# Softmax sums of a head pair: reciprocals spread on VectorE and transposed, instead of broadcast by matmuls

## The chip, the cores and the metric

One NeuronCore of a Trainium2 chip runs the whole program. The metric is the device time of one execution in microseconds. The kernel before was timed in three runs, with a median of 2175.9 us.

## The reference, cut to what matters

The program is three transformer layers over 512 tokens of width 1024, in float32. Each has an attention part of several heads of width 64 and a feed-forward part. What the change touches is the end of each head's softmax attention:

```
logits = q @ k.T (+ decay, + causal mask)          # [queries, keys] of one head
p = softmax(logits, axis=-1)                       # exp(logits - max) / sum
out = p @ v                                        # [queries, 64]
```

In the last layer a learned sink adds exp(sink - max) to the sum; there and in the heads over a memory of 256 tokens the rest is the same.

## The kernel before, in words

Heads are worked off in 22 pairs, in three stages: 8 pairs from about 60 to 270 us of the span (stage 1: two over the memory, six causal ones), 8 from about 700 to 870 us (stage 2, the same numbers) and 6 from about 1655 to 1780 us (stage 3, four windowed ones with sinks and two over the memory). Between the stages lie the feed-forward parts, which the change does not touch.

A pair is two heads x = 0, 1 and 512 queries, four blocks of 128. Its key blocks are grouped into units of up to 512 score columns (128 for the causal pairs of stage 2, 256 in stage 3), and `Pairs.run` (L890) gives TensorE its work in rounds, a software pipeline of three steps. In a round it issues the scores of one unit (`score`, L786), and then, by `older` (L881), the values of the unit scored two rounds ago (`values`, L845) and the turn of the unit scored one round ago (`turn`, L816: transposes of the exponentials in float32, L1732). When the unit whose values are due is its pair's last (`sealed`), the round also has the pair's sums (`sums`, L854). In stages 1 and 2 the sums stand first, ahead of the values; in stage 3, where every job has `spare` set, they stand last, behind the turn. Rounds are interleaved with the dense matmuls of the layer (`beat`, L445, which lets side work through at a set pace), and `after(n, ...)` puts a step on the other engines' lists n units of model time later. All engines walk the one list `steps` in order, each with its own instructions; waits are on counting semaphores.

For a pair, VectorE takes the row maxima (L1895, scaled at L1904), ACT the exponentials with their sums as an accumulated output into `PSTAT[:, x, 1, i]` (L2139), TensorE turns the exponentials into PSUM, and ACT and VectorE copy them back to SBUF (L2146 and L1917; where `spare` is set, ACT alone copies both heads). With the turn of the last unit `copies` (L828) first orders `recip` (L868, step `precip`) and then these copies, so that on VectorE the reciprocal (L1927) stands directly ahead of the copy L1917. It makes 128x8 numbers: per query row of a block, 2 heads x 4 blocks. The step `pbcast` (L1750) then brings them into the layout of the output, [64 dimensions of head x, 512 queries], by eight matmuls per pair: the stationary operand is a column of reciprocals broadcast to 64 columns, the moving one is the identity. ACT copies the result to one of three buffers TMP (step `pspread`, L2162), VectorE multiplies the values in PSUM bank 6 by it (step `pmul`, L1932), ACT and VectorE split the product into a high and a low part (L2151, L1935). The values of the next pair start once L1932 has read bank 6. PSTAT has two buffers, handed on by `pstats`; TMP's three by `tmp`.

Other instructions that the prediction speaks of: the split of the weights into two parts on ACT and VectorE (L2069, L1795), three units of four tiles ahead of their use (`split_to`, L525); the normalisation of keys (L1849) and its transposes (`qturn`, L1684); the dense matmuls with three terms for each tile (L1625 to L1627, L1643 to L1645).

Of the kernel before, what the change touches and what calls it, by code (L numbers as in the profile page):

```python
# [287 lines left out]
def program(nc, io):  # L288
    with ExitStack() as ctx:
# [25 lines left out]
        IDENT, ONES2 = CONST[:, 0:128], CONST[:, 128:130]  # L315
# [24 lines left out]
        TMP = [sb(f"TMP{i}", [128, T]) for i in range(3)]  # L340
# [42 lines left out]
        PSTAT = [sb(f"PSTAT{i}", [128, 2, 4, 4]) for i in range(2)]  # L383
        GATE = [sb(f"GATE{i}", [128, 4, 12]) for i in range(2)]
        PSA = ctx.enter_context(nc.psum_tensor("PSA", [128, 8, T], F32))
        PS = [PSA[:, i, :] for i in range(8)]
# [11 lines left out]
        done = Signals(nc, ctx, now)  # L398
# [89 lines left out]
        sq, tmp, cv, gf, ys, ss, pstats, pp, pt = (Slots(n, need) for n in (2, 3, 4, 2, 2, 2, 2, 4, 2))  # L488
        ring, aux_ring, att_ring, held = [0, 1], [6, 7], [2, 3, 4, 5, 7], set()

        def step(kind, key, **a):
            if (kind, key) in WARM:
                warm((kind, key), WARM[kind, key])
            steps.append(Step(kind, key, a))
            for name in RAISES[kind]:
                done.mark(name, key)
# [272 lines left out]
        class Pairs:  # L769
# [16 lines left out]
            def score(self, n, u):  # L786
                job, key, jkey = self.jobs[n], (self.id, n, u), (self.id, n)
                if u == 0:
                    pstats.take(jkey, [("pbcast.pe", jkey)])
                self.at[key] = t = Unit(job.units[u], pick_pair(att_ring), job.spare)  # L790
                held.update(t.banks)
                for x, b in enumerate(t.banks):
                    psum.take(("pscore", key, x), [("pexp.act", key + (x,))], b)
                step("pscore", key, job=job, u=u, t=t)
                S, tokens = PSTAT[pstats.of[jkey]], pstats.before[jkey]

                def rest():
                    need(job.roots[1] if job.roots else [])
                    for xs in ((slice(0, 2),) if t.joint else (slice(0, 1), slice(1, 2))):
                        step("pmax", key + (xs.start,), job=job, t=t, xs=xs, S=S, tile=key, before=tokens)  # L800
                    if job.sealed(u) and job.sink is not None:
                        step("psink", jkey, job=job, S=S, last=key + (0 if t.joint else 1,))
                    after(0.8 if job.spare else 0, exponents)

                def exponents():
                    free = []
                    for n_ in range(t.parts):
                        t.P.append(pp.take(("pp", key, n_), [("pturn.pe", key + (x,)) for x in range(2) if t.shared or x == n_]))
                        free += pp.before["pp", key, n_]
                    for x in range(2):  # L810
                        step("pexp", key + (x,), job=job, t=t, x=x, S=S, P=t.of(PP, t.P, x), before=tokens, src=PS[t.banks[x]],
                             turned=free, top=("pmax.dve", key + (0 if t.joint else x,)))
                after(0.4, rest)
                return 0.4 + 1.4 * t.width / 512
# [39 lines left out]
            def sums(self, n, i):  # L854

                jkey, ckey = (self.id, n), (self.id, self.jobs[n].chunk)
                need([("precip.dve", jkey)])
                aux = aux_bank(("pbcast", jkey), [("pspread.act", ckey)])
                step("pbcast", jkey, S=PSTAT[pstats.of[jkey]], bank=aux)

                def spread():
                    x = tmp.take(("pmix", ckey), [("pmix.dve", ckey)])
                    step("pspread", ckey, jkey=jkey, bank=aux, F=TMP[x], before=tmp.before["pmix", ckey])
                    after(0.1 if self.jobs[n].spare else 0.4, lambda: self.mix(n))
                after(0.3, spread)
                return 0.8

            def recip(self, n):  # L868
                job, jkey = self.jobs[n], (self.id, n)
                S = PSTAT[pstats.of[jkey]]  # L870
                step("precip", jkey, job=job, S=S, last=self.end(n))

            def mix(self, n):
                job, key = self.jobs[n], (self.id, self.jobs[n].chunk)
# [6 lines left out]
            def older(self, scored, turned):  # L881

                ends = turned and self.jobs[turned[0]].sealed(turned[1])
                late = ends and self.jobs[turned[0]].spare
                cost = self.sums(*turned) if ends and not late else 0
                cost += self.values(*turned) if turned else 0
                cost += self.turn(*scored) if scored else 0
                return cost + (self.sums(*turned) if late else 0)

# [411 lines left out]
        last, norm = norm, Norm("mix1", XT, "mix1")  # L1301
# [46 lines left out]
        for p in range(6):  # L1348
            w = places[p % 2]
# [23 lines left out]
        for gr in range(3):  # L1373
# [71 lines left out]
            for x in range(2):  # L1445
                p = 2 * gr + x
# [162 lines left out]
        def tensor(pe):  # L1609
            w = Once(pe)  # L1610
            for s in steps:
# [114 lines left out]
                elif k == "pturn":  # L1726
                    for t in a["before"]:
                        w.wait_ge(*done(*t))
                    w.wait_ge(*done("pexp.act", key))
                    for x in range(a["t"].width // 128):  # L1730
                        c = slice(128 * x, 128 * x + 128)
                        p = pe.transpose(a["out"][:, c], a["P"][:, c], IDENT)  # L1732
                    p.then_inc(done.sem("pturn.pe"), 1)
                elif k == "pvals":
                    job, tile = a["job"], a["t"]
                    if a["u"] == 0:
                        for t in psum.before["pvals", a["jkey"]]:
                            w.wait_ge(*done(*t))
                    for t in tile.copied:
                        w.wait_ge(*done(*t))  # L1740
                    for i, col, k0, nk, masks in tile.subs:
                        nb = nk // 128
                        for j in range(nb):
                            for x in range(2):
                                r = slice(64 * x, 64 * x + 64)
                                p = pe.matmul(PS[6][r, 128 * i:128 * i + 128], job.v[:, k0 // 128 + j, r],
                                              tile.of(PT, tile.PT, x)[:, col + 128 * j:col + 128 * j + 128], start=(j == 0),
                                              stop=(j == nb - 1))
                    p.then_inc(done.sem("pvals.pe"), 1)
                elif k == "pbcast":  # L1750
                    for t in psum.before["pbcast", key]:
                        w.wait_ge(*done(*t))
                    w.wait_ge(*done("precip.dve", key))
                    for i in range(4):
                        for x in range(2):
                            p = pe.matmul(PS[a["bank"]][64 * x:64 * x + 64, 128 * i:128 * i + 128],
                                          a["S"][:, x, 3, i:i + 1].broadcast_to([128, 64]), IDENT, start=True, stop=True)
                    p.then_inc(done.sem("pbcast.pe"), 1)
                elif k == "warm":
                    w.wait_ge(s_cb, 16)  # L1760
                    for t in psum.before["warm", key]:
                        w.wait_ge(*done(*t))
                    for _ in range(a["n"]):
                        pe.matmul(PS[a["bank"]][:, 0:384], IDB, CB[:, 0:384], start=True, stop=True)
                elif k == "centre":
                    out = PS[a["bank"]][:, :]
                    for t in psum.before["centre"]:
                        w.wait_ge(*done(*t))
                    w.wait_ge(*done("tap.dve", (1, 29)))
                    pe.matmul(out, ONES, CA[0], start=True, stop=False)  # L1770
                    pe.matmul(out, ONES, CA[1], start=False, stop=True).then_inc(done.sem("centre.pe"), 1)
                elif k == "spreadout":
                    out = PS[a["bank"]][:, :]
                    for t in psum.before["spreadout"]:
                        w.wait_ge(*done(*t))
                    w.wait_ge(*done("lnsquare.act", 0))
                    pe.matmul(out, ONES, SG[0], start=True, stop=False)
                    pe.matmul(out, ONES, SG[1], start=False, stop=True).then_inc(done.sem("spreadout.pe"), 1)

        def vector(dve):  # L1780
# [6 lines left out]
            for s in steps:  # L1787
# [130 lines left out]
                elif k == "precip":  # L1918
# [3 lines left out]
                    if a["job"].sink is not None:  # L1922
# [1 line left out]
                        dve.tensor_tensor(St[:, :, 1, :], St[:, :, 1, :], St[:, :, 2, :],  # L1924
                                          ALU.add).then_inc(v_in.sem, v_in.up())
                        w.wait_ge(v_in.sem, v_in.n)
                    dve.reciprocal(St[:, :, 3, :], St[:, :, 1, :]).then_inc(done.sem("precip.dve"), 1)  # L1927
                elif k == "pmul":
                    F = a["F"][:, :]
                    w.wait_ge(*done("pvals.pe", a["last"]))  # L1930
# [507 lines left out]
```

## Time and profile before

| | |
|---|---|
| median of three runs | 2175.9 us (2173.77 to 2177.2) |
| profiled execution | 2173.69 us, span 2171.9 us |
| granted TensorE clock, mean | 0.995 |
| TensorE busy (matmuls) | 2106.6 us, 97% |
| TensorE busy (weight loads) | 1749.7 us, 81% |
| VectorE busy | 1268.6 us, 58% |
| ScalarE (ACT) busy | 938.9 us, 43% |
| GpSimd busy | 33.9 us, 2% |
| DMA | 86 GB/s over the span |

Busy times of an engine are sums over its records. The records of consecutive instructions of one engine overlap, since they are pipelined: what an instruction costs its engine is read from the distance between its start and the next one's. PE are TensorE's matmuls and PEld its weight loads, which run ahead of the matmuls that they belong to. A float32 matmul has two records, a float32 transpose one. In an engine's rows an idle time stands in brackets, with the instruction that ended it; "issue" is idle time in which it waited for nothing that the profile shows. The granted clock is a share of 2.4 GHz.

### The profile page before, as it was taken

How to read it: one execution, taken by the hardware profiler on the slowest of the kernel's cores; microseconds unless marked ns; L12 is line 12 of the kernel's file. 1: busy time of each engine (PE TensorE's matmuls, PEld its weight loads, DVE VectorE, ACT ScalarE, POOL GpSimd, SP SyncE). 2: the span in 40 equal slices, each digit the busy share in tenths (PEclk: the TensorE clock that was granted, in tenths of full speed). 3: DMA queues.
4: the chain of work that ended last, by engine and by line, in shares of the span. 5: the costliest groups of instructions: out<-in, count | busy, mean ns of one | idle time of the engine just before them, and what ended most of it. 6: DMA issues, size and time to landing. Idle time of an engine off the chain costs nothing. (4 is left out here: it accounts for less than half of the span.)

```text
span 2171.9 us, 30675 instructions
## 1 busy us (share of the span) xinstructions
PE 2106.6 (97%) x11441; PEld 1749.7 (81%) x11441; DVE 1268.6 (58%) x2133; ACT 938.9 (43%) x1898; POOL 33.9 (2%) x71
## 2 busy tenths in 40 slices
PE   7999999999999898999999999999999889999999
PEld 7899777888889676788888888888888667888887
DVE  7655567737755775776477544344448856443542
ACT  7655444424445764543244343223344654322331
POOL 0000001000001000000000000000001000000000
PEclk9999999999999999999999999999999999999999
DMA  6221123332233011233322323323332112333332
GB/s 214 79 59 54 50 78 97 107 97 88 97 98 97 16 35 35 74 102 103 91 97 97 102 93 98 101 92 98 97 96 65 30 45 88 97 99 96 97 97 93
DMA packets 101669, 187.36 MB, mean 86 GB/s; under 512 B 11408, under 2 KB 12048, under 8 KB 101264
## 3 DMA queue, kind: packets, MB, share of 16 engines
q1 hardware_dynamic: 101520, 185.39, 27.6%
q8 instruction: 91, 1.49, 0.3%
q14 instruction: 58, 0.48, 0.1%
HBM read 183.25 MB, written 2.10 MB: 85 GB/s over the span
## 5 line engine op out<-in xcount | busy, mean ns | idle before, releaser
L1795 DVE TENSOR_TENSOR WL<-RAW,WH 128x512 fp32r<-128x512 f32 x681 | 458.7, 690 | 357.9 <-ACT WH L2069 336.5
L1625 PE MATMUL PSA<-HNh,WH 128*128 128x512 f32 x1440 | 563.8, 392 | 5.6 <-DVE HNl L1784 4.2
L1627 PE MATMUL PSA<-HNh,WL 128*128 128x512 f32 x1440 | 560.3, 389 | 0.0
L1626 PE MATMUL PSA<-HNl,WH 128*128 128x512 f32 x1440 | 560.3, 389 | 0.0
L2069 ACT ACTIVATE WH<-RAW 128x512 fp32r<-128x512 f32 x681 | 413.1, 625 | 312.7 <-PE PSA L1627 221.3
L1625 PEld LDWEIGHTS PSA<-HNh,WH 128*128 128x128 f32 x1440 | 270.3, 188 | 66.7 <-DVE HNl L1784 7.6
L1627 PEld LDWEIGHTS PSA<-HNh,WL 128*128 128x128 f32 x1440 | 270.3, 188 | 56.8
L1626 PEld LDWEIGHTS PSA<-HNl,WH 128*128 128x128 f32 x1440 | 270.3, 188 | 56.6 <-issue 1.2
L1625 PE MATMUL PSA<-Gh,WH 128*128 128x512 f32 x704 | 274.1, 389 | 2.1 <-DVE Gl L1964 2.1
L1626 PE MATMUL PSA<-Gl,WH 128*128 128x512 f32 x704 | 273.9, 389 | 0.0
L1627 PE MATMUL PSA<-Gh,WL 128*128 128x512 f32 x704 | 273.9, 389 | 0.0
L1818 DVE TENSOR_TENSOR PSA<-PSA,ACC 128x512 f32<-128x512 f32 x180 | 125.3, 697 | 118.3 <-PE PSA L1627 111.9
L1784 DVE SCALAR_TENSOR_TENSOR CV<-PSA,PAR,CV 128x511 f32<-128x511 f32 (+1 forms) x176 | 131.9, 749 | 77.9 <-ACT CV L2168 74.7
L1643 PE MATMUL PSA<-WH,HNh 128*128 128x256 f32 (+2 forms) x512 | 153.0, 299 | 12.6 <-DVE HNl L1784 7.2
L2186 ACT ACTIVATE Gh<-GF 128x512 fp32r<-128x512 f32 x88 | 55.7, 633 | 235.1 <-DVE GF L1962 235.1
L1625 PEld LDWEIGHTS PSA<-Gh,WH 128*128 128x128 f32 x704 | 132.1, 188 | 30.2 <-DVE Gl L1964 2.9
L1626 PEld LDWEIGHTS PSA<-Gl,WH 128*128 128x128 f32 x704 | 132.1, 188 | 27.5
L1627 PEld LDWEIGHTS PSA<-Gh,WL 128*128 128x128 f32 x704 | 132.1, 188 | 27.4
L1644 PE MATMUL PSA<-WH,HNl 128*128 128x256 f32 (+2 forms) x512 | 148.4, 290 | 0.0
L1645 PE MATMUL PSA<-WL,HNh 128*128 128x256 f32 (+2 forms) x512 | 148.2, 289 | 0.0
L2168 ACT ACTIVATE CV<-PSA,PAR 128x512 f32<-128x512 f32 x88 | 68.6, 780 | 181.0 <-DVE PSA L1818 181.0
L1784 DVE SCALAR_TENSOR_TENSOR XT<-PSA,XT 128x512 f32<-128x512 f32 x64 | 44.3, 692 | 142.4 <-PE PSA L1627 142.4
(255 smaller groups left out, 2439.0 us busy)
## 6 DMA issues: line engine op xcount, KB each, us to landing
RAW<-in_w SPq DMA_DIRECT2D x681, 256.0 KB, 2.6
XT<-in_x SPq DMA_DIRECT2D x8, 256.0 KB, 5.2
MT<-in_mem SPq DMA_DIRECT2D x2, 1024.0 KB, 6.9
out_x<-XT SPq DMA_DIRECT2D x8, 256.0 KB, 2.0
PAR<-in_par SPq DMA_DIRECT2D x1, 207.0 KB, 7.2
CB<-in_cb SPq DMA_DIRECT2D x1, 100.0 KB, 7.2
PAR<-in_par SPq DMA_DIRECT2D x1, 84.5 KB, 2.0
CONST<-in_const SPq DMA_DIRECT2D x1, 65.0 KB, 5.7
```

The source lines that it names most:

```text
L1625: pe.matmul(out, wh, xh, start=(a["start"] and c == 0), stop=False)
L1626: pe.matmul(out, wh, xl, start=False, stop=False)
L1627: p = pe.matmul(out, wl, xh, start=False, stop=ends)
L1643: pe.matmul(out, h[:, c], wh, start=(a["start"] and t % a["share"] == 0), stop=False)
L1644: pe.matmul(out, l[:, c], wh, start=False, stop=False)
L1645: p = pe.matmul(out, h[:, c], wl, start=False, stop=(a["stop"] and t % a["share"] == a["share"] - 1))
L1784: ins = dve.scalar_tensor_tensor(*x)
L1795: dve.tensor_tensor(l[:, :], r[:, :], h[:, :], ALU.subtract).then_inc(done.sem("split.dve"), 1)
L1818: dve.tensor_tensor(ps, ps, nm.acc, ALU.mult).then_inc(done.sem("scale.dve"), 1)
L2069: act.activation(h[:, :], r[:, :], ACT.Copy).then_inc(done.sem("split.act"), 1)
L2168: act.activation(CV[cv.of[key]][:, :], PS[a["bank"]][:, :], ACT.Identity, bias=par(f"cb{a['layer']}", a["idx"]), scale=par(f"cw{a['layer'] ...
L2186: act.activation(Gh[:, a["q"], :], G[:, :], ACT.Copy).then_inc(done.sem("gated.act"), 1)
```

## The change

The reciprocal writes 128x512 numbers in place of 128x8: each of the eight columns is spread over 64 columns of a TMP buffer by a broadcast input. Four transposes of 128x128 bring that into the output's layout, in place of the eight matmuls. TMP is now taken twice for each pair (by `recip` and by `spread`), PSTAT is free once the reciprocal has read it, and in `older` the sums are behind the values where they were ahead of them. Nothing else is changed.

```diff
--- before.py
+++ after.py
@@ -786,7 +786,7 @@
             def score(self, n, u):
                 job, key, jkey = self.jobs[n], (self.id, n, u), (self.id, n)
                 if u == 0:
-                    pstats.take(jkey, [("pbcast.pe", jkey)])
+                    pstats.take(jkey, [("precip.dve", jkey)])
@@ -856,7 +856,7 @@
                 need([("precip.dve", jkey)])
                 aux = aux_bank(("pbcast", jkey), [("pspread.act", ckey)])
-                step("pbcast", jkey, S=PSTAT[pstats.of[jkey]], bank=aux)
+                step("pbcast", jkey, inv=TMP[tmp.of["inv", jkey]], bank=aux)
@@ -868,7 +868,8 @@
             def recip(self, n):
                 job, jkey = self.jobs[n], (self.id, n)
                 S = PSTAT[pstats.of[jkey]]
-                step("precip", jkey, job=job, S=S, last=self.end(n))
+                i = tmp.take(("inv", jkey), [("pbcast.pe", jkey)])
+                step("precip", jkey, job=job, S=S, inv=TMP[i], before=tmp.before["inv", jkey], last=self.end(n))
@@ -882,8 +883,8 @@
                 ends = turned and self.jobs[turned[0]].sealed(turned[1])
                 late = ends and self.jobs[turned[0]].spare
-                cost = self.sums(*turned) if ends and not late else 0
-                cost += self.values(*turned) if turned else 0
+                cost = self.values(*turned) if turned else 0
+                cost += self.sums(*turned) if ends and not late else 0
                 cost += self.turn(*scored) if scored else 0
                 return cost + (self.sums(*turned) if late else 0)
@@ -1752,9 +1753,8 @@
                         w.wait_ge(*done(*t))
                     w.wait_ge(*done("precip.dve", key))
                     for i in range(4):
-                        for x in range(2):
-                            p = pe.matmul(PS[a["bank"]][64 * x:64 * x + 64, 128 * i:128 * i + 128],
-                                          a["S"][:, x, 3, i:i + 1].broadcast_to([128, 64]), IDENT, start=True, stop=True)
+                        c = slice(128 * i, 128 * i + 128)
+                        p = pe.transpose(PS[a["bank"]][:, c], a["inv"][:, c], IDENT)
                     p.then_inc(done.sem("pbcast.pe"), 1)
@@ -1924,7 +1924,11 @@
                         w.wait_ge(v_in.sem, v_in.n)
-                    dve.reciprocal(St[:, :, 3, :], St[:, :, 1, :]).then_inc(done.sem("precip.dve"), 1)
+                    for t in a["before"]:
+                        w.wait_ge(*done(*t))
+                    dve.reciprocal(a["inv"][:, :].rearrange("p (i x d) -> p i x d", i=4, x=2),
+                                   St[:, :, 1, :].rearrange("p x i -> p i x").unsqueeze(3).broadcast_to(
+                                       [128, 4, 2, 64])).then_inc(done.sem("precip.dve"), 1)
```

## Rows read from the trace of the kernel before

**Rows 1.** The page's head and the busy time of each engine.
```profile
span 2171.9 us, 30675 instructions
...
PE 2106.6 (97%) x11441; PEld 1749.7 (81%) x11441; DVE 1268.6 (58%) x2133; ACT 938.9 (43%) x1898; POOL 33.9 (2%) x71
```

**Rows 2.** Busy time by stretch: PE, PEld, DVE, ACT, POOL, clock, DMA share, GB/s.
```profile
60.00:300.00 240.00, 237.52 (x2002) 207.98 (x1999) 132.51 (x256) 127.66 (x329) 0.00 (x0) 1.00 0.21 61
700.00:880.00 180.00, 159.16 (x1204) 125.83 (x1202) 118.26 (x228) 108.50 (x285) 11.60 (x11) 0.97 0.11 32
1655.00:1790.00 135.00, 118.62 (x925) 89.27 (x924) 103.84 (x234) 77.31 (x203) 6.01 (x9) 0.97 0.13 38
```

**Rows 3.** TensorE's weight loads in order of time (start, duration), first pair: sums, values, turns.
```profile
75.48 0.85 PEld L1756 LDWEIGHTS PSA<-CONST,PSTAT 128*64 128x64 f32 x16
76.30 0.91 PEld L1746 LDWEIGHTS PSA<-PT,VMEM 128*64 128x64 f32 x16
77.38 0.86 PEld L1732 LDWEIGHTS PSA<-CONST,PP 128*128 128x128 f32 x8 [0.17 <-issue]
```

**Rows 4.** The same view around four transposes of another step.
```profile
133.72 0.46 PEld L1684 LDWEIGHTS PSA<-CONST,YB 128*128 128x128 f32 x4
134.15 0.19 PEld L1643 LDWEIGHTS PSA<-WH,HNh 128*128 128x128 f32 x1
```

**Rows 5.** Groups by line: duration in ns as min/median/max, first and last start.
```profile
L1756 PE MATMUL PSA<-CONST,PSTAT x352: 272/273/324, 75.5 to 1777.9; 128*64 128x128 f32 x176
...
L1927 DVE RECIPROCAL PSTAT<-PSTAT x22: 193/202/205, 71.5 to 1775.7; 128x8 f32<-128x8 f32 x22
...
L1836 DVE TENSOR_SCALAR SS<-SS x31: 158/165/189, 37.4 to 1721.8; 128x8 f32<-128x8 f32 x25, 128x16 f32<-128x16 f32 x6
```

**Rows 6.** Costliest groups of the page: the weights' low part on VectorE.
```profile
L1795 DVE TENSOR_TENSOR WL<-RAW,WH 128x512 fp32r<-128x512 f32 x681 | 458.7, 690 | 357.9 <-ACT WH L2069 336.5
```

**Rows 7.** VectorE in order of time around the first pair's reciprocal.
```profile
71.46 0.17 DVE L1904 TENSOR_TENSOR PSTAT<-PSTAT,QR 128x4 f32<-128x4 f32 x1
71.54 0.20 DVE L1927 RECIPROCAL PSTAT<-PSTAT 128x8 f32<-128x8 f32 x1
71.66 0.67 DVE L1917 COPY PT<-PSA 128x512 f32<-128x512 f32 x1
```

**Rows 8.** Stage 3, first pair: VectorE's reciprocal and TensorE's first sum.
```profile
1684.99 0.20 DVE L1927 RECIPROCAL PSTAT<-PSTAT 128x8 f32<-128x8 f32 x1
...
1685.93 0.20 PEld L1756 LDWEIGHTS PSA<-CONST,PSTAT 128*64 128x64 f32 x4 [0.17 <-issue]
```

**Rows 9.** Stages 1 and 2: reciprocals and first sums of three pairs; a wait for YK.
```profile
157.93 0.20 DVE L1927 RECIPROCAL PSTAT<-PSTAT 128x8 f32<-128x8 f32 x1
...
159.15 1.09 PE L1756 MATMUL PSA<-CONST,PSTAT 128*64 128x128 f32 x16
...
769.76 0.39 PEld L1684 LDWEIGHTS PSA<-CONST,YK 128*96 128x96 f32 x4 [0.58 <-DVE YK L1849]
...
813.80 0.20 DVE L1927 RECIPROCAL PSTAT<-PSTAT 128x8 f32<-128x8 f32 x1
...
814.20 1.09 PE L1756 MATMUL PSA<-CONST,PSTAT 128*64 128x128 f32 x16
...
866.27 0.19 DVE L1927 RECIPROCAL PSTAT<-PSTAT 128x8 f32<-128x8 f32 x1
...
867.32 0.88 PE L1756 MATMUL PSA<-CONST,PSTAT 128*64 128x128 f32 x12
```

**Rows 10.** Waits of TensorE, and two stretches behind them (columns as in rows 2).
```profile
712.43 0.42 PEld L1732 LDWEIGHTS PSA<-CONST,PP 128*128 128x128 f32 x4 [3.93 <-ACT PP L2139]
...
714.00:716.00 2.00, 2.00 (x13) 1.61 (x13) 1.93 (x4) 1.37 (x4) 0.00 (x0) 0.50 0.04 8
...
1714.00:1717.00 3.00, 3.00 (x21) 2.23 (x21) 1.36 (x7) 1.69 (x5) 0.00 (x0) 0.50 0.00 0
```

**Rows 11.** What TensorE (PE and PEld together) waited for before L1746: us, times.
```profile
  DVE TMP L1932: 7.7, 8
```

## The prediction

> **What bounds the kernel now.** I read the page's first part, then the busy time by stretches. TensorE is busy for 97% of the span [rows 1], and the three stretches in which the 22 pairs of heads run are 240, 180 and 135 us long; TensorE is busy for 237.5 of the first, but only 159.2 and 118.6 of the others, where VectorE is busy for two thirds and more [rows 2]. So TensorE's order of instructions is the time: every microsecond that one of its instructions takes, or waits, shows one to one, and VectorE costs nothing until something that TensorE needs is late. Then I read the instructions in order of time around each pair's end, on TensorE (to see what the sums and their neighbours take) and on VectorE (to see how soon after the reciprocal TensorE comes for something that stands behind it).
>
> **TensorE's part: what is removed.** A pair's sums are 8 matmuls with 64 columns of weights, 16 records; 22 pairs give the 352 records of their group [rows 5]. The sixteen take from 75.48 to 76.30, where the values start: 0.82 us [rows 3]. Four transposes of the same 128x128 float32 form, in another step, hold the engine from 133.72 to 134.15: 0.43 us [rows 4]. By the weight loads' starts that is 0.39 us less for a pair, by the matmuls' starts 0.5; I take 0.45, times 22: 9.9 us. A change between matmuls and transposes shows as an idle time of 0.17 us [rows 3]. In the first 16 pairs (stages 1 and 2) the sums now go between values and turns: values, then 0.17, then sums and turns without a gap, against values, 0.17, turns before: nothing changes. In the last 6 (the third stage) the sums already stood behind the turns, and stay there; only their form changes, and the 0.17 before them [rows 8] goes, and mostly the one behind them too: about 1.7 us together. **TensorE's saving: 11 to 12 us, taken as 11.5.** Without anything else the kernel would take 2162.2.
>
> **VectorE's part: what is added.** The reciprocal of 128x8 becomes one of 128x512. No row shows a reciprocal of that size. Any 128x512 instruction with two operands takes 0.69 us [rows 6], so 0.6 us from start to start is the least. But the small reciprocal is not like its neighbours: it takes 0.202 us where a tensor_scalar on 128x8 takes 0.165 [rows 5], and the instruction behind it starts 0.12 us after it, where the one behind a 128x4 tensor_tensor starts 0.08 us after [rows 7]. A longer pipeline alone would lengthen the record, not the distance to the next start. Read as work for each element, with some 0.07 us fixed: (0.12 - 0.07)/8 = 6.2 ns by the starts, and (0.202 - 0.157)/8 = 5.6 by the durations, where 1.04 ns is the rate of a plain instruction ((690 - 165)/504) [rows 5, 6]. 512 elements then take 2.9 to 3.3 us; I take **3.2 us from start to start, 3.1 more than now**. The rows leave 0.6 (all of the excess fixed) to 3.9 us (the starts are rounded to 0.01). I take the value of the rows and not the low end because both the duration and the distance carry the same excess. 22 x 3.1 is 68 us of VectorE. PSTAT's buffers come free a little earlier, and TMP's three buffers are now taken twice per pair; the buffer's last reader is a pair back, so I cost both at nothing: what covers it is that a pair lasts for many times the 0.6 us by which any of them comes later. No DMA is added or moved, and SP and POOL see nothing.
>
> **What stands behind the reciprocal.** In stages 1 and 2 it is the copy of the transposed probabilities (L1917, 0.69 us), which the pair's last values need. The values now go where the sums started. So TensorE waits wherever its first sum started less than 3.2 + 0.69 = 3.9 us after the reciprocal did. Distances in the 16 pairs, in order of time: 3.9, 3.9, 2.2, 1.2, 5.5, 1.5, 3.0, 2.5, 2.0, 1.0, 2.1, 3.1, 3.8, 0.4, 2.1, 1.1. The first stands in [rows 3, 7] (71.54 to 75.48), two more and the last in [rows 9]: 157.93 to 159.15, a stall of 2.7 us; 813.80 to 814.20, 3.5; 866.27 to 867.32, 2.8. The sum over the 16 is 24.6 us. In one pair the chain behind the reciprocal is worse than its copy: TensorE already waited for VectorE's YK at 769.76 [rows 9], so the whole 3.1 us comes through there and not 0.7: 2.3 more. In the third stage ACT makes the copies, but the sums themselves wait for the reciprocal's 3.2 us; distances 0.9, 2.0, 3.0, 3.0, 3.5, 1.5 (the first: 1684.99 to 1685.93 [rows 8]): 5.9 us. **Direct stalls: 32.8 us.** The weight splits behind it on VectorE are ordered three units of weights (twelve tiles) ahead, and I let that hide them; without that cover they would wait as long as the copies do.
>
> **Second terms.** The sums' copy to SBUF (L2162) and the product (L1932) come about 0.6 us later in stages 1 and 2, since the values go first. TensorE waited 8 times for L1932 [rows 11]: about 2 us more. The clock: behind a wait of 3.9 us the granted clock was 0.50 for a stretch at 714 us, which is 1.2 of 2.4 GHz, and it was 0.50 again from 1714 us, behind several shorter ones [rows 10]. Stalls of about 3 us will do this at a few more places; a stretch of 2 to 3 us at half speed gives back 1 to 1.5. I take 5 us, bounds 0 and 12. Against this, waits for the exponentials that stand now behind some of these places shrink: 4 us off. **Sum: 32.8 + 2 + 5 - 4 - 11.5 = 24.3 us slower.** The profiled execution took 2173.7 (its span of 2171.9 and 1.8 around it); the median of the three runs is 2.2 above it. 2173.7 + 24.3 = 2198, 2200 by the median; I say **2199**.
>
> **Rivals.**
> (a) Cheap reciprocal, and so faster. The excess of 0.04 us is fixed for each instruction, and 128x512 takes 0.6 to 0.7 us. Place: VectorE, line 1927. The distances under 0.6 + 0.69 = 1.3 are then four, with 1.5 us of stalls together, and the later product costs 2: 11.5 - 3.5 = 8 gained, 2166. It decides below about 1.7 us a reciprocal, where stalls and saving cancel. For it: 8 elements are a short lever for 512. Against it: the distance to the next start has grown as well. Chance 0.14.
> (b) Dearer reciprocal: eight times the plain rate, 8 x 1.04 = 8.3 ns an element, 4.3 us. Each of the stalls grows by 1.1 us and three more pairs stall, about 24 us more: 2223. Against it: 8 elements would then have cost 0.058 us more than a plain instruction, and 0.04 was seen. Chance 0.11. The Trainium skill (VectorE: DVE Perf Modes, the section on the pipeline walkthrough) says that Reciprocal is an iterative divide on two of the eight slices with a repeat count of 8. By that rule, read as eight cycles an element, (b) would be the forecast; the trace's small reciprocal agrees with the direction and not with the full eight.
> (c) Right price, but TensorE finds it hidden: VectorE's copies catch up because the waits of one stall push back what competes with the next, and half of the 32.8 us is not seen; no clock lost. 16 + 2 - 4 - 11.5 = 3: 2178. For it: VectorE is busy for only 55% of stage 1. Against it: the distances are between two instructions that nothing else separates. Chance 0.11.
> That the change moves no values is no rival: TensorE runs its steps in the order written.
>
> **How the numbers follow.** The forecast's case (2 to 3.9 us a reciprocal, stalls seen) has 0.64 and by itself runs from about 2184 to 2215. 0.2% is about 4.3 us, which is what a measurement of this kernel can tell from no change. Faster: (a) and little of (c), 0.16. Within: part of (c), 0.06. Slower: 0.78. The range of 8 in 10 starts in (c), at 2176, and ends at 2222, just short of (b)'s middle.
>
> **What would show it.** The reciprocal's group: near 3.2 us a record (0.7 for (a), 4.3 for (b)). Transposes in place of the sums: 88 records, about 0.43 us for four, placed behind the values. TensorE's idle time before L1746 with VectorE's PT as its releaser: near 25 us in stages 1 and 2, where the product is the only releaser worth the name now [rows 11]; and before the sums of the third stage some 6 us with TMP as releaser. More stretches with a clock of 0.50 in stage 2. VectorE's total near 1335 us. The prediction is wrong if the reciprocal's record is under 1.7 us, or if it is about 3 and TensorE's idle time has not grown by more than 12 us.

## The result, and the profile after

Four runs of the changed kernel have a median of 2224.0 us (2223.2 to 2226.2), beside 2174.8 us for four runs of the kernel before: a ratio of 1.0226, 95% interval 1.0214 to 1.0239. The change costs 49 us; the forecast was 24, and 2224 lies just above its range. The profiled execution took 2224.45 us.

The page's head and busy times of the changed kernel, to be held against [rows 1]:

```profile
span 2222.7 us, 30151 instructions
...
PE 2115.4 (95%) x11177; PEld 1755.0 (79%) x11177; DVE 1334.9 (60%) x2133; ACT 938.4 (42%) x1898; POOL 34.8 (2%) x71
```

VectorE has 66 us more, as forecast (1335). TensorE executes 264 instructions fewer and is nevertheless busy for 9 us longer. The busy times by stretch (columns as in [rows 2], stages 1 to 3, somewhat longer stretches since the stages are) tell why: the granted clock of stages 2 and 3 fell to 0.91, and in stage 1, where it stays at 0.99, TensorE is idle for 14.3 us of 240 instead of 2.5.

```profile
60.00:300.00 240.00, 225.72 (x1854) 197.41 (x1852) 147.86 (x242) 122.82 (x322) 0.00 (x0) 0.99 0.21 58
700.00:900.00 200.00, 163.61 (x1106) 130.62 (x1104) 139.71 (x229) 110.70 (x292) 12.03 (x11) 0.91 0.10 29
1680.00:1820.00 140.00, 115.37 (x846) 89.42 (x845) 120.19 (x241) 75.75 (x200) 9.86 (x14) 0.91 0.13 37
```

The new reciprocal's group (ns min/median/max):

```profile
L1929 DVE RECIPROCAL TMP<-PSTAT x22: 3342/3353/3354, 71.0 to 1825.0; 128x512 f32<-128x512 f32 x22
```

VectorE in order of time around the fourth pair's reciprocal, the pair of 157.93 and 159.15 in [rows 9]:

```profile
160.12 3.35 DVE L1929 RECIPROCAL TMP<-PSTAT 128x512 f32<-128x512 f32 x1
163.39 0.63 DVE L1917 COPY PT<-PSA 128x512 f32<-128x512 f32 x1
```

and TensorE's weight loads behind it, values and transposes:

```profile
164.13 1.58 PEld L1747 LDWEIGHTS PSA<-PT,VP 128*64 128x64 f32 x16 [2.68 <-issue]
166.04 0.72 PEld L1757 LDWEIGHTS PSA<-CONST,TMP 128*128 128x128 f32 x4 [0.33 <-issue]
```

The copy starts 3.27 us after the reciprocal (160.12 to 163.39) and the values start 4.01 us after it, 2.68 us after TensorE was ready: the stall that the forecast gave this pair (2.7). The view calls the releaser "issue" for the weight loads and PT L1917 for the matmuls of the same records. The sixteen loads then take 1.58 us where they took 0.91 in [rows 3]: from 164 to 166 us the granted clock was 0.56, half clock for most of that stretch. The waits of TensorE's weight loads by line and releaser (us in total, times, longest), after:

```profile
PEld PSA L1747 <- issue: 27.8, 20, 4.0
PEld PSA L1733 <- ACT PP L2143: 24.3, 37, 3.9
...
PEld PSA L1713 <- DVE PT L1917: 9.4, 7, 2.7
...
PEld PSA L1757 <- DVE TMP L1929: 6.8, 4, 2.6
...
PEld PSA L1713 <- DVE HNl L1784: 4.0, 3, 1.8
...
PEld PSA L1747 <- DVE TMP L1936: 3.7, 3, 2.1
PEld PSA L1685 <- DVE YK L1849: 3.7, 1, 3.7
...
PEld PSA L1713 <- DVE AOL L1784: 3.4, 1, 3.4
PEld PSA L1757 <- issue: 3.4, 15, 0.3
...
PEld PSA L1747 <- DVE PT L1917: 2.0, 1, 2.0
```

and before, from the same view (lines one lower; L1746 are the values, L1732 the turns, L1712 the scores, L1684 the Q and K turns):

```profile
PEld PSA L1732 <- ACT PP L2139: 21.6, 37, 3.9
...
PEld PSA L1746 <- DVE TMP L1932: 4.3, 4, 2.0
...
PEld PSA L1712 <- DVE PT L1917: 3.6, 5, 1.5
...
PEld PSA L1712 <- DVE HNl L1784: 2.6, 3, 1.2
...
PEld PSA L1746 <- issue: 2.6, 9, 0.4
...
PEld PSA L1684 <- DVE YK L1849: 1.7, 2, 1.1
...
PEld PSA L1712 <- DVE AOL L1784: 0.4, 1, 0.4
```

**Two accounts.** For each kernel I take TensorE's idle time (the span less its busy time) and, from the view of busy times in stretches of 1 us, its "clock loss", the sum of (1 - granted clock) x busy time: what its busy time would shrink by at the full clock of 2.4 GHz. Before: 65.3 idle, 9.1 clock loss. After: 107.3 and 28.8. The rest, TensorE's work at full clock, went from 2097.5 (2106.6 - 9.1) to 2086.6. So +42.0 idle, +19.7 clock loss and -10.9 of work are the 50.8 us by which the spans differ. This account says where the time lies, not what it would give back.

Work hangs together by stage; where a stage ends is read from the first matmul of the next normalisation's total (L1668 before, L1669 after). All kernels of this case; the medians are of all their runs, the other columns of one profiled execution each, which can lie a few us from its median (e3's was the fastest of ten runs, e13's the slowest of eleven, 2175.5 us):

| kernel | median us | stage 1 ends | stage 2 ends | stage 3 ends | idle | clock loss |
|---|---|---|---|---|---|---|
| before | 2174.8 | 308.7 | 898.6 | 1819.4 | 65.3 | 9.1 |
| after | 2224.0 | 318.5 | 936.1 | 1870.2 | 107.3 | 28.8 |
| e1_order_only | 2178.2 | 307.9 | 902.4 | 1823.2 | 66.5 | 11.0 |
| e2_form_only | 2215.4 | 313.4 | 930.7 | 1862.8 | 100.8 | 25.9 |
| e3_copy_spread | 2176.9 | 304.5 | 898.3 | 1819.8 | 72.8 | 12.3 |
| e4_pool_spread | 2174.7 | 305.6 | 901.2 | 1822.5 | 69.1 | 20.4 |
| e5_form_copy | 2176.4 | 304.9 | 896.4 | 1821.0 | 70.3 | 16.8 |
| e6_dummy_block | 2230.5 | 319.5 | 939.3 | 1875.4 | 110.8 | 32.3 |
| e7_copy_first | 2212.7 | 310.8 | 921.6 | 1855.9 | 98.6 | 22.9 |
| e8_warm_fill | 2225.0 | 316.4 | 936.3 | 1871.3 | 85.7 | 25.6 |
| e9_form_fill | 2168.8 | 305.1 | 896.4 | 1816.2 | 58.0 | 8.0 |
| e10_before_fill | 2169.6 | 307.8 | 895.1 | 1815.9 | 52.4 | 3.4 |
| e11_half_block | 2193.0 | 309.6 | 911.2 | 1838.1 | 85.8 | 17.8 |
| e12_after_fill_more | 2221.7 | 316.6 | 929.8 | 1865.8 | 73.0 | 7.3 |
| e13_form_stage1 | 2172.7 | 305.9 | 898.2 | 1821.2 | 64.2 | 15.8 |
| e14_form_stage1_fill | 2168.7 | 304.9 | 895.5 | 1816.3 | 52.6 | 6.6 |

The kernel before had medians of 2174.2 to 2175.2 us beside these groups of runs; ratios below are against those.

### The profile page after: what moved, and what is told of

The parts are those of the page before. It is cut to its first block and busy times, and to the rows that moved or that the text cites. A ratio compares the mean times of both kernels' runs of the same rounds, so it can differ in the third digit from the quotient of the medians.

```text
span 2222.7 us, 30151 instructions
## 1 busy us (share of the span) xinstructions
PE 2115.4 (95%) x11177; PEld 1755.0 (79%) x11177; DVE 1334.9 (60%) x2133; ACT 938.4 (42%) x1898; POOL 34.8 (2%) x71
```

## The experiments

**The two halves of the change, each alone.** The order alone in the kernel before, and the new form alone in the changed one:

```diff
# e1_order_only: before, with
-                cost = self.sums(*turned) if ends and not late else 0
-                cost += self.values(*turned) if turned else 0
+                cost = self.values(*turned) if turned else 0
+                cost += self.sums(*turned) if ends and not late else 0
# e2_form_only: the change, with these lines the other way round
```

> The kernel before with one edit: the sums stand behind the values; reciprocal of 128x8 and eight matmuls stay. Block theory (the loss comes from the reciprocal's 3.35 us on VectorE, 22 times, which makes TensorE wait and then lets its clock fall): the order alone costs what the later product costs, 1 to 3 us, 2176 to 2178. Order theory (the loss is the order's: product late, next pair's values late): 2190 or more. Clock: no more stretches at 0.50 than before under the block theory.

> The changed kernel with the old order: sums ahead of values, the long reciprocal and the four transposes stay. Block theory: the sums now wait for the reciprocal's 3.35 us and the values still for the copy 0.67 us later, so the waits are the same but for the 0.4 us of transposes that now fill a part: 2216 to 2224. Order theory: back by 20 us or more, under 2205.

Measured: 2178.2 us, ratio 1.0023 (1.0012 to 1.0034), and 2215.4 us, ratio 1.019 (1.0173 to 1.0207). The order by itself costs 4 to 5 us; the form by itself 41 of the 49. With the long reciprocal the new order adds 8.6 us.

**The same form without the long reciprocal.** The reciprocal stays at 128x8, and a copy spreads it over 64 columns each:

```diff
# e3_copy_spread
-                    dve.reciprocal(<inv>, <sums, broadcast>).then_inc(done.sem("precip.dve"), 1)
+                    dve.reciprocal(St[:, :, 3, :], St[:, :, 1, :]).then_inc(v_in.sem, v_in.up())
+                    w.wait_ge(v_in.sem, v_in.n)
+                    dve.tensor_copy(<inv>, <St 3, broadcast>).then_inc(done.sem("precip.dve"), 1)
# e4_pool_spread: the copy on GpSimd, pbcast waits for that
# e5_form_copy: e3 with the old order, sums first
```

> The changed kernel, but the reciprocal is of 128x8 again and a copy on VectorE spreads it to 128x512 (0.2 + about 0.6 us from start to start in place of 3.35); transposes, order and buffers as changed. Block theory: the saving of 11.5 us shows, less 2 to 4 for the later product and short waits: 2165 to 2170, clock stretches as before. Rival (transposes beside transposes lose the clock, or the order costs): 2185 or more with clock stretches at 0.50 in all stages.

> As the copy-spread kernel, but the spreading copy is GpSimd's, which has nothing else to do there: about 1.3 us a copy, off VectorE. Block theory: 2163 to 2170, at or under the copy on VectorE, unless the sums wait for GpSimd in pairs where they follow the reciprocal within 1.7 us; there up to 1 us each, 5 us at most. Rival as for the copy-spread kernel: 2185 or more.

> Sums ahead of values as before, reciprocals of 128x8, a VectorE copy that spreads them (0.43 us), four transposes. If the order of the change is what costs about 4 us by itself (as the run with the order alone had +4 against the kernel before) and the two effects add, 2176.9 - 4 = 2173 us, idle time of TensorE near 68 us. If the four transposes' saving of 11.5 us reached the end once the order is old, 2166 us. A result of 2177 or more says that the order is worth nothing beside the transposes.

Measured: 2176.9 us, ratio 1.0016 (1.0006 to 1.0025); 2174.7 us, ratio 1.0004 (0.9995 to 1.0014); 2176.4 us, ratio 1.0008 (0.9998 to 1.0017). VectorE in order of time in e3, first pair:

```profile
70.85 0.20 DVE L1927 RECIPROCAL PSTAT<-PSTAT 128x8 f32<-128x8 f32 x1
71.08 0.43 DVE L1931 COPY TMP<-PSTAT 128x512 f32<-128x512 f32 x1
71.43 0.68 DVE L1917 COPY PT<-PSA 128x512 f32<-128x512 f32 x1
```

The block ahead of the copy is 0.58 us in place of 3.27, and 47 of the 49 us are gone: they hang on the block, not on the transposes. (The 0.58 us is from the start of the reciprocal to that of the copy L1917.) But nothing is gained on the kernel before either. TensorE's work at full clock fell to 2086.4 us in e5 (2103.2 busy less 16.8), 11.1 below before; 5.0 more idle and 7.7 more clock loss take it back. The order is worth nothing measurable here (2176.9 and 2176.4).

**Is it the reciprocal, or the time on VectorE?** The short reciprocal with seven copies in a chain:

```diff
# e6_dummy_block: e3, with ahead of its copy
+                    for _ in range(6):
+                        dve.tensor_copy(<inv>, <St 3, broadcast>).then_inc(v_in.sem, v_in.up())
+                        w.wait_ge(v_in.sem, v_in.n)
```

> The change, but with a reciprocal of 128x8 and seven spreading copies one behind the other in its place, each waiting for the last: a VectorE block of about 3.2 us that holds no long reciprocal. Theory (the time goes to what is queued on VectorE behind the block, and to the clock that falls behind these waits): 2219 to 2228 us, the same as the changed kernel, with the waits before the values at 1.4 to 4 us again. Rival (the reciprocal itself disturbs something, a port or a buffer, or the 2 KB result held in TMP does): close to the run with one copy, 2177 us.

Measured: 2230.5 us, ratio 1.0252 (1.0235 to 1.027), with these rows of VectorE:

```profile
70.92 0.20 DVE L1927 RECIPROCAL PSTAT<-PSTAT 128x8 f32<-128x8 f32 x1
71.16 2.74 DVE L1932 COPY TMP<-PSTAT 128x512 f32<-128x512 f32 x6
73.94 0.43 DVE L1934 COPY TMP<-PSTAT 128x512 f32<-128x512 f32 x1
74.28 0.68 DVE L1917 COPY PT<-PSA 128x512 f32<-128x512 f32 x1
```

3.36 us from 70.92 to 74.28, against 3.27, and 6.5 us above the changed kernel, more than a block longer by 0.09 us explains; why is not shown. The values' wait is 30.0 us in its view of waits. A block on VectorE at this place that holds no long reciprocal costs as much as the long reciprocal, so the rival, something particular to the reciprocal, is out.

**How the cost grows with the block.** Half the reciprocal, and a copy for the other half:

```diff
# e11_half_block: the change, with
+                    V = a["inv"][:, :].rearrange("p (i x d) -> p i x d", i=4, x=2)
+                    dve.reciprocal(V[:, :, :, 0:32], <sums, broadcast to 32>)
+                    dve.tensor_copy(V[:, :, :, 32:64], V[:, :, :, 0:32])
```

> The change with a reciprocal of 128x256 and a copy that doubles its columns. The reciprocal should take 1.65 to 1.75 us (half of 3.35, if the price goes by the element), the block about 2.1 us against 0.6 with the small reciprocal (2176.9 us) and 3.3 with the full one (2224.0 us). A cost that goes in proportion to the block gives 2176.9 + 47 * 1.5 / 2.7 = 2203 us; if short blocks are covered by the slack of the copies (about 1 us ahead of the values), 2190 us.

Measured: 2193.0 us, ratio 1.009 (1.0076 to 1.0104). VectorE's rows:

```profile
71.86 1.75 DVE L1930 RECIPROCAL TMP<-PSTAT 128x256 f32<-128x256 f32 x1
73.65 0.29 DVE L1933 COPY TMP<-TMP 128x256 f32<-128x256 f32 x1
73.86 0.69 DVE L1917 COPY PT<-PSA 128x512 f32<-128x512 f32 x1
```

The price goes by the element: (3.35 - 1.75)/256 = 6.25 ns. The time does not go in proportion: blocks of 0.58, 2.0 and 3.27 us give 2176.9, 2193.0 and 2224.0 us, 11 us for each us of block at first and 24 behind that. The prediction's distances, read at those blocks, make direct stalls of about 1, 14 and 33 us: steps of 13 and 19, where 16 and 31 were measured.

**The reciprocal behind the copies instead of ahead of them:**

```diff
# e7_copy_first: the change, in copies()
-                    if job.sealed(u):
-                        self.recip(n)
                     ...
+                    if job.sealed(u):
+                        self.recip(n)
```

> The change with its reciprocal issued behind the round's copies instead of ahead of them. Theory: the values of the last round no longer wait (their copies are ahead of the block), which gives back the 25 to 28 us of idle before the values; but the sums, 1 to 3 us behind the values, now wait for the reciprocal, and the next pair's maxima, queued behind it, make the next exponentials late. Expected 2195 us (2185 to 2215), with the idle time before the sums' transposes up from 7 to some 20 us and less of the clock lost (15 us against 29). Rival: only the place where the block lies changes, the total of waits does not: 2220 us or more.

Measured: 2212.7 us, ratio 1.0173 (1.0158 to 1.0188), 11 us better than the change and 38 worse than before. Its waits:

```profile
PEld PSA L1757 <- DVE TMP L1929: 18.6, 12, 2.6
...
PEld PSA L1685 <- DVE YK L1849: 5.6, 2, 3.6
...
PEld PSA L1747 <- issue: 4.4, 15, 0.4
...
PEld PSA L1713 <- DVE PT L1917: 2.5, 4, 1.1
```

The values' 27.8 us are back at 4.4 and the scores' 9.4 at 2.5, and the sums take their place with 18.6. That score steps lose their wait on PT together with the values shows where it came from: by `turn` (L816) and the scores' bank pick, the copy L1917 also frees the PSUM banks of the turned exponentials for later scores. The forecast had not counted that.

**The clock.** The kernel already has `warm` steps: bf16 matmuls of 128x384 into a free bank (L1764), whose results nobody reads. I put more of them in front of steps that wait, by adding to the table of them:

```diff
# e8_warm_fill: the change, with 8 to 19 at 11 values and 3 sums (two entries shown)
+        ("pvals", (0, 3, 2)): 13, ("pbcast", (2, 0)): 13,
# e12_after_fill_more: e8, with 9 to 22 more at nine other waits
# e9_form_fill: e5, e10_before_fill: before, both with
-        ("pturn", (1, 0, 0, 0)): 14,
+        ("pturn", (1, 0, 0, 0)): 36, ("pscore", (1, 2, 0)): 9, ("pscore", (1, 6, 1)): 15, ("pscore", (2, 0, 3)): 10,
+        ("pscore", (2, 2, 1)): 6, ("pvals", (2, 2, 0)): 6, ("pturn", (2, 2, 1, 0)): 9, ("pvals", (2, 5, 0)): 14,
```

(A ninth entry, left out above, found no free bank and puts nothing in: the wait of 3.1 us at one score step of stage 2 stays. In e12 three entries of the table put nothing in either; the nine are those that do.)

> The change with 8 to 19 bf16 matmuls of 128x384 (0.16 us each) ahead of the values that wait 1.4 us or more for their copies (11 pairs), and ahead of three sums of the last stage: they fill the waits and change no wait. Theory (some 20 of the 50 us are the clock that falls after these waits): the clock loss falls from 29 us to 12 to 18, the time from 2224 to 2208 to 2214 us. Rival (the low clock has another cause, or only follows from low load over the whole stage): 2222 to 2230 us.

> The change with the fills of the run that filled the values' waits (2225.0 us, clock loss 26 us) and nine more, 9 to 22 matmuls each, in front of other waits of 1.6 to 3.9 us that lie ahead of its remaining stretches at half clock (first exponentials of stage 2, a K split, two score steps, three in stage 3). Theory (the clock falls where waits of several kinds lie close together, so filling one kind alone did not keep it): clock loss 15 us or less, time 2209 to 2214 us. Rival (in the changed kernel the low clock covers only time that it would wait in any case): 2220 us or more with the clock loss down as well. If the clock loss stays above 20 us, the fills do not steer it and its share stays open.

> The form with the small reciprocal, one copy and four transposes in the old order (the run before: 2176.4 us, 70 us of idle and 17 us of clock loss), with 6 to 22 more bf16 matmuls of 128x384 in front of eight waits of 1.2 to 3.9 us that lie ahead of its stretches at half clock. Theory (the low clock follows these waits and holds the end back, so it is what eats the 11.5 us of the transposes): clock loss 7 us or less, time 2164 to 2169 us, a version that beats both kernels. Rival (the clock loss moves elsewhere or replaces waiting for ScalarE): 2173 to 2180 us.

> The kernel before with the same fills at the same steps. Its clock loss is 9 us only. By the theory 2167 to 2171 us; by the rival 2172 to 2178 us. If both filled kernels come down by the same amount, the fill and not the form is what helps.

Measured: e8 2225.0 us, ratio 1.0227 (1.0212 to 1.0242); e12 2221.7 us, 1.0219 (1.0202 to 1.0236); e9 2168.8 us, 0.997 (0.9961 to 0.9979); e10 2169.6 us, 0.9981 (0.9973 to 0.999). At nine of its eleven values a fill of e8 does what it should where it stands: TensorE is busy until about the time that the copy is there.

```profile
160.85 2.29 PE L1770 MATMUL PSA<-CB 128*128 128x384 bf16 x13
163.52 1.09 PE L1753 MATMUL PSA<-PT,VP 128*64 128x128 f32 x16 [0.38 <-DVE PT L1923]
```

At the other two (the third and the seventh pair of stage 2, here the third) the fill's own bank is one that the late copy frees. The fill waits for the copy itself, and then the values wait for the fill, 2.8 us longer than they needed to:

```profile
766.84 0.88 PEld L1770 LDWEIGHTS PSA<-CB 128*128 128x128 bf16 x6 [1.95 <-DVE PT L1923]
...
769.62 1.43 PEld L1753 LDWEIGHTS PSA<-PT,VG 128*64 128x64 f32 x16 [0.62 <-issue]
```

The low clock behind the first place is gone (the values take 1.09 us), yet over the kernel the clock loss only fell from 28.8 to 25.6, since it came up behind other waits. In e12 it did fall, to 7.3; stages 2 and 3 read

```profile
700.00:900.00 200.00, 176.26 (x1252) 134.53 (x1251) 140.79 (x229) 109.50 (x290) 12.04 (x11) 0.98 0.10 30
1680.00:1820.00 140.00, 123.61 (x918) 91.56 (x916) 117.28 (x234) 75.89 (x202) 8.74 (x12) 0.96 0.12 35
```

and the kernel is hardly faster, 2.3 us. The added matmuls are 51 us of work (busy 2145.3 less 7.3, against 2086.6); idle time and fill together are 124 us against 107.3 idle, so 17 of the 21.5 us of clock loss came back as waiting or as fill. About half of those 17 us are the fills' own doing. In e12 the two misplaced ones hold the values up by 1.7 us each, and in stage 3 two outlast the wait that they stand in. The plainest stands ahead of a score whose last release, an ACT copy, ended at 1753.81 us:

```profile
1753.23 0.58 ACT L2159 ACTIVATE PT<-PSA 128x512 f32<-128x512 f32 x1
...
1754.32 3.26 PE L1773 MATMUL PSA<-CB 128*128 128x384 bf16 x19
1757.51 0.33 PE L1722 MATMUL PSA<-BKH,BQH 64*128 64x128 f32 x2
```

That is 3.2 us of delay; the other, ahead of a turn at 1814.2 us that was released at 1812.4, makes 1.8. Together 8.5 us in four fills, so the gain of 2.3 us doesn't price the clock: it is a lower bound, and 2.3 + 8.5, about 11 of the 21.5 us, is my estimate if these delays count in full. In the kernels with little waiting it is otherwise: in e10 5.7 us less clock loss went with 5.3 us (medians beside each other, 2174.9 and 2169.6), in e9 8.8 us less with 7.6. Both are faster than the kernel before, and e9 and e10 differ by less than their intervals can tell.

Runs of one and the same kernel say something too, since each has its granted clock. Of the 81 runs of the kernel before that stand beside these experiments, the four with a clock of 0.993 took 2177.0 us in the mean and the 21 with 0.996 took 2172.6: 4.4 us for some 6.5 us of clock loss. The runs of e8, where TensorE waits much, took 2226.7 us at 0.986 and 2221.0 at 0.990. The two move together in both, which doesn't say which drives the other.

**Where the transposes' saving is lost.** The form of e5 in stage 1 only (`self.id == 0`), the eight matmuls in the other stages; e14 with the fills of e9:

```diff
# e13_form_stage1, e14_form_stage1_fill
+                        if a["inv"] is None:      # stages 2 and 3
+                            for x in range(2):
+                                p = pe.matmul(<64 columns of head x, block i>, <reciprocals, broadcast>, IDENT, ...)
+                            continue
```

> The form with the small reciprocal, one copy and four transposes (old order) in the 8 pairs of stage 1 alone; the other 14 pairs as before. Theory (in stage 1 TensorE sets the pace and 8 x 0.5 us come through; in stages 2 and 3 the saving turns into waits and some 2 to 4 us more are lost): 2170.5 to 2172 us, against 2176.4 us for the form in all stages. Rival (the saving is spread evenly and lost by chance of the clock): 2174.5 to 2177 us.

> The same with the fills of the two filled kernels (2168.8 us with the form everywhere, 2169.6 us with it nowhere). By the ends of the stages in those two profiles (stage 1: 305.1 against 307.8 us; stage 2: 591.3 against 587.2 us long) the mixture should take 2166 to 2167 us, and beat both by 2 to 3 us; by the rival it lies between them, 2169 us.

Measured: 2172.7 us, ratio 0.9987 (0.9978 to 0.9996), and 2168.7 us, ratio 0.9972 (0.9961 to 0.9982). Without fills the mixture is 3.7 us faster than the form everywhere, a better time than the rival gave and 0.7 us slower than the theory's interval; with them it is equal to e9, as the rival had it. In all six kernels with the cheap form there, stage 1 ends 2.8 to 4.2 us earlier than before. Part of that is a stretch at half clock that lies ahead of the first pair, where no kernel was changed; the kernel before has it, e1 has not (columns as in [rows 2]):

```profile
41.00:45.00 4.00, 3.98 (x20) 3.98 (x21) 3.35 (x12) 1.76 (x6) 0.00 (x0) 0.57 0.59 168
...
41.00:45.00 4.00, 3.74 (x30) 3.65 (x31) 3.54 (x12) 1.76 (x5) 0.00 (x0) 1.00 0.41 126
```

Held like with like, e4 and e13 with that stretch against before, the other four against e1 and e10 without it, stage 1 ends 2.7 to 3.5 us earlier, and its work is 2.9 us less in e5. That much comes through. In stages 2 and 3 the lengths don't follow the work. Stage 2 has the same instructions of attention in before, e13, and (but for fills) in e10 and e14: 589.9, 592.3, 587.2 and 590.5 us, with a clock loss there of 4.1, 7.6, 1.7 and 4.9 us. In each pair the later figure is 2.4 or 3.3 us longer with 3.5 or 3.2 us more clock loss. So 3 us in stage 2 go with the clock's stretches, and that much and the saving of a stage are alike. Whether the stretches move because stage 1 ends at another time, or come and go between executions as the one near 42 us does, one trace of each kernel can't say. Stage 3 gives one comparison at the same clock loss, 1.7 us in both: e9 has 4.0 us less work there than e10, 3.0 us more idle time, and ends 1.0 us sooner. With the clock held fully up in all stages it was not tried.

## Why the prediction was right and wrong

- **The bound**: right in the main. TensorE's order set the time, and VectorE's 66 us cost what they made TensorE wait.
- **TensorE's saving, 11.5 us: this step failed as time**, though right as work (10.9). e3, e4 and e5 have it and would be at 2164 or so by this step; they take 2175 to 2177. Stage 1's part, about 3 us for 8 pairs, reaches that stage's end, and the form in stage 1 alone (e13) is 2.5 us faster than before. The prediction said that "every microsecond that one of its instructions takes, or waits, shows one to one", with the figures for stages 2 and 3 beside it (159.2 of 180 us, 118.6 of 135) that say otherwise: where TensorE waits for a tenth of the time, a saving can become waiting, as 3.0 of 4.0 us did in stage 3 between e10 and e9.
- **The reciprocal, 3.2 us**: right, 3.27 from start to start and 3.35 a record. The excess of a 128x8 record was per element. That it came so near has some luck in it: starts are rounded to 0.01 us, which is 0.6 us on 512 elements, and the two readings gave 2.9 and 3.2. Rival (a) is out, and so is (b)'s price of 4.3 us, though its time of 2223 is the one measured: it had the wrong mechanism with the right sum. By the rule of the Trainium skill (VectorE: DVE Perf Modes, the pipeline walkthrough), read as eight cycles an element at the plain rate of 1.04 ns, the record would be 4.3 us, an estimate; the trace shows 6.25 ns an element, six times the plain 1.04, so the measurement decides against that reading.
- **Direct stalls, 32.8 us**: right. The values wait 27.8 + 2.0 in place of 2.6 (+27.2, forecast 24.6), YK's turn 3.7 in place of 1.7 (+2.0, forecast 2.3), the sums 6.8 + 3.4 in place of 3.6 in three small rows (+6.6, forecast 5.9): 35.8 us.
- **Second terms, 2 - 4 us: this step failed, and with the wrong sign.** The waits for exponentials did not shrink by 4 us but grew by 2.7 (24.3 against 21.6). Scores waited 5.8 us more for PSUM banks that L1917 frees (9.4 against 3.6), 3.0 more for one split (AOL) and 1.4 for others (HNl); the later product cost nothing (3.7 against 4.3). That is +12.3 where -2 was forecast. With other small waits less, the idle time is 42.0 us up against a forecast of 30.8. Not all of it is the block's, as the same rows of e3 show, which has the change without the block:

```profile
PEld PSA L1733 <- ACT PP L2143: 23.5, 42, 3.9
...
PEld PSA L1713 <- DVE HNl L1784: 4.3, 3, 2.0
...
PEld PSA L1713 <- DVE PT L1917: 2.6, 5, 1.1
...
PEld PSA L1713 <- DVE AOL L1784: 0.6, 1, 0.6
```

  What comes with the block is the banks and the AOL split, 6.8 and 2.8 us, and both are things that it holds up in VectorE's queue: the copy L1917, and a split right behind the reciprocal of a pair of stage 3:

```profile
1764.94 3.35 DVE L1929 RECIPROCAL TMP<-PSTAT 128x512 f32<-128x512 f32 x1 [0.29 <-DVE PSTAT L1924]
1768.21 0.65 DVE L1784 SCALAR_TENSOR_TENSOR AOL<-PSA,PAR,AOH 128x512 fp32r<-128x512 f32 x1
```

  The prediction let the splits be hidden and did not count the banks. e7 is the test of the banks: with the copies first, that wait is 2.5 us. By e11 a us of direct stall cost 1.2 us for short blocks (16 for 13) and 1.6 for long ones (31 for 19), the clock's part included.
- **The clock, 5 us (bounds 0 and 12)**: the stretches came, at 12 places instead of 5, and by the account 19.7 us more lie in them, which is four times the term. e12 takes 21.5 us of it away and gains 2.3 us, but its fills delay four steps by 8.5 us. How much of the 49 us is the clock stays open between 2 and some 20 us.
- **The sum.** Between e3 and the changed kernel, which differ by the block alone, 47.1 us were measured where the forecast has 35.8 (24.3 + 11.5); between before and e3, +2.1 where it has -11.5. These two gaps, 11.3 and 13.6 us, are the 24.9 us that were missing. The second is the saving that was taken as time: in e3's trace 7.5 us more idle time and 3.2 more clock loss stand against 10.3 less work. The first is the block's: 34.5 us more idle time where the forecast had 30.8, and 16.5 more clock loss where it had 5. Which of the two makes up the 11.3 us stays open with the price of the clock.
- **Rival (c)**, stalls hidden by half: the opposite happened.

## What to carry to other kernels

An instruction with no row of its own can be priced from a small one by its excess over like neighbours, in duration and in distance to the next start, when both carry it; this is one case, and the rounding left a wide range. A block put ahead of a queue on a helper engine costs the direct stalls and, beyond them, what its late copies hold: list the buffers and banks that each queued instruction frees, not only who reads its result; here a stall cost 1.2 to 1.6 times itself. A matmul put in to fill a wait needs a bank that the late instruction doesn't free, and a length that ends before the wait does; look at both in the trace before reading its effect. A saving on the engine that bounds the time counts fully only in stretches where that engine has no idle time; spread a few numbers with a plain copy rather than compute each 64 times.

## What was not expected of the hardware

- A reciprocal on VectorE costs 6.25 ns an element and about 0.15 us fixed in its record: 0.20 us for 128x8, 1.75 for 128x256, 3.35 for 128x512. A copy that broadcasts 128x8 to 128x512 takes 0.43 us, less than the 0.69 of a two-operand instruction [rows 6]; on GpSimd it took 0.65.
- Half clock (1.2 GHz) came and went at the same instructions: near 42 us, ahead of all that was changed, it is in the traces of before, e4, e11 and e13 and in none of the other twelve, and in stage 2 the same instructions had 4.1 or 7.6 us of clock loss. Filling 14 waits with matmuls removed it at some places and it appeared at others; only with nine more of different kinds did it fall, from 25.6 to 7.3 us. Removing it went with nearly its own size where TensorE waited little (5.3 us for 5.7, 7.6 for 8.8). Where it waited for VectorE, 2.3 us came back for 21.5, with 8.5 us of delay by the fills themselves in between.
- The two kernels with the cheap form and fills (e14, e9) are the fastest seen, 2168.7 and 2168.8 us, 0.3% below the kernel before. Nearly all of that is the fills': the kernel before with them takes 2169.6.
